# Latent heads of the attention: halves of the output copied by ScalarE and joined by a product with stacked identities

## The chip, the cores and the metric

The kernel runs on one core of a Trainium2 chip. The time is the device time of one execution in microseconds (us), the median of several runs.

## The reference, cut to what matters

One layer of an encoder is computed for two sequences of 512 rows with 1024 columns each: norm and input projection, two groups of attention heads, output projection and residual, then a mixture of 16 experts. Only the attention matters here. It has 16 heads per sequence: 8 grouped-query heads (64 columns, two key/value heads) and 8 latent heads (64 columns plus 32 rotary ones for queries and keys, 64 columns for values, each with keys and values of its own).

```python
def one_block(qblk):
    sc = jnp.einsum('bqkgd,bskd->bkgqs', qblk, k).astype(jnp.float32) * scale
    p = jax.nn.softmax(sc, axis=-1).astype(v.dtype)
    return jnp.einsum('bkgqs,bskd->bqkgd', p, v)
```

## The kernel before

**Stages.** The first stage (project) makes the rows of queries, keys and values of both sequences, the second (attend) does the attention of all 32 heads, g = 0 to 31: the first sequence's 8 grouped and 8 latent heads, then the second's (SETS = 2, HEADS = 16, QH = MH = 8). The third (route) does the output projection, the residual, the norm and the choice of rows for each expert, the fourth the experts.

**Units.** A unit of the attention is one block of 128 queries of one head against its 512 keys, so a head has TS = 4 units and there are NU = 128. Each engine runs through the same counter u, written out by hand, and does for each u one step of several units that are at different ages; semaphores join the engines. For unit u TensorE computes the scores (L1086 and L1087 in grouped heads, three products L1089 to L1091 in latent ones), VectorE takes the negated maximum (L1275), ScalarE the exponential (L1214), TensorE transposes the probabilities (L1100), ScalarE copies them in a rounded format, the high part (L1223), VectorE subtracts it from the transposed probabilities, the low part (L1269). Before a new head, queries and, where it has its own, keys are transposed (L1073) and split in the same way (L1182 to L1188 on ScalarE, L1239 to L1249 on VectorE).

**Values.** Two units at a time, TensorE multiplies values and probabilities (function values, L1118 and L1121). The stationary operand of L1118 has 128 columns, the high part of the values beside their low part. So the bank of PSUM called OT_BANK holds, for one head, 64 rows (0 to 63) from the high part of the values and 64 rows (64 to 127) from the low part, each 512 queries long, and the head's output is the sum of the two, still transposed.

**Joining the halves.** Grouped heads (g % 16 < 8): at u = 4 g + 9 ScalarE copies all 128 rows to the tile ot (L1204) and raises ot_added; at u = 4 g + 10 TensorE multiplies four blocks of it with halves, two 64 x 64 identities one above the other (L463 makes it), which adds the halves and turns them in one (L1133). Latent heads: at u = 4 g + 9 ScalarE copies the lower half to the tile otv (L1206) and raises ot_copied; VectorE adds the upper half from PSUM (L1259, in add_halves, called ahead of the low part of the probabilities, or behind it in the last steps), and raises ot_added; at u = 4 g + 10 TensorE transposes four blocks of 64 rows with an identity (L1135). In both, VectorE then scales the result by the reciprocal of the row sums (L1284, L1287), and SyncE stores groups of heads to HBM.

**Order around it.** On TensorE, in one u: preparations, scores of u, transposes of the probabilities of u - 3, output of a head (u = 4 g + 10), values (u even). Near the end, from u = 125 on, the output projection's first transposes (L1426) and products (L1444) stand in between. The first value product of head g waits until ot_added has counted the g heads before it. Outputs therefore come out some ten steps late: those of heads 6 and 7 (and 22 and 23) while latent heads are scored, those of heads 13 to 15 while grouped heads of the second sequence begin.

Of the kernel before, what the change touches and what calls it, by code (L numbers as in the profile page):

```python
# [16 lines left out]
ALU = mybir.AluOpType  # L17
# [101 lines left out]
def build(nc, a, out):  # L119
# [11 lines left out]
    with ExitStack() as ctx:  # L131
# [107 lines left out]
        att["pthi"] = [Map(shared_at)("probThi0", [P, TS, 2 * P], F32R), bm("probThi1", [P, TS, 2 * P], F32R)]  # L239
        att["v"] = [bm(f"v{i}", [P, TS, 2, VD], F32R) for i in range(2)]  # L240
        att["ot"] = bm("ot", [P, SEQ])
        att["otv"] = bm("otv", [VD, SEQ])
        assert bm.at <= w_in_end, (bm.at, w_in_end)

        om = Map(weights_at)
# [682 lines left out]
def attend(phase, project_signals, a, k, att, wo, ps, banks, o_rows, o_stored, wo_loaded):  # L928
# [23 lines left out]
        due.setdefault(max(0, TS * (g - 1) + (0 if kind == "k" else 2)) if g else -1, []).append((kind, g))  # L952
    PREP, S_BANKS, T_BANKS, OT_BANK, O_BANK = 0, (1, 2, 3), (4, 5), 6, 7
    PAIRS = NU // 2
    pthi, ptlo, ot, otv = (att[n] for n in ("pthi", "ptlo", "ot", "otv"))

    sem = phase.sem
    prep_ready, prep_hi, prep_lo = sem("prep_ready"), sem("prep_hi"), sem("prep_lo")
    score_ready, max_done, exp_done = sem("score_ready"), sem("max_done"), sem("exp_done")
    pt_ready, pthi_done, ptlo_done, pv_done = sem("pt_ready"), sem("pthi_done"), sem("ptlo_done"), sem("pv_done")  # L960
    vhi_done, vlo_done, ot_copied, o_ready, ot_added = sem("vhi_done"), sem("vlo_done"), sem("ot_copied"), sem("o_ready"), sem("ot_added")
    rsum_done, o_done = sem("rsum_done"), sem("o_done")
    wo_hi, wo_scaled, wo_lo = sem("wo_hi"), sem("wo_scaled"), sem("wo_lo")

# [92 lines left out]
    def tensor_program(pe, first_key, finish_tile, o_transposes, product, route_rest):  # L1057
        def prepare(kind, g):
            n = prep_index[kind, g]
            pj, q_rows, kv_rows = rows_of(g)  # L1060
            h = g % HEADS
            if kind == "k":
                wait_for_rows(pe, g)
            if n:
                pe.wait_ge(prep_lo, n)
            for i in range(TS):
                if h < QH:
                    c = h * HD if kind == "q" else C_K + h // GROUP * HD
                    src, dst = pj[:, i, c:c + HD], ps[0:HD, PREP, i * P:(i + 1) * P]
                else:  # L1070
                    src = q_rows[:, i, h - QH, :] if kind == "q" else kv_rows[:, i, h - QH, 0:QK]
                    dst = ps[0:QK, PREP, i * P:(i + 1) * P]
                last = pe.transpose(dst, src, k["ident"][:])  # L1073
            last.then_inc(prep_ready, 1)

        def scores(u):
            g, i = units[u]
            if i == 0:
                pe.wait_ge(prep_lo, prep_index["q", g] + 1)
            if u >= 3:  # L1080
                pe.wait_ge(exp_done, u - 2)
            elif u:
                pe.wait_ge(row_copied, T)
            dst, q, kk, cols = ps[:, S_BANKS[u % 3], :], g % 2, key_of[g] % 2, slice(i * P, (i + 1) * P)
            if g % HEADS < QH:
                pe.matmul(dst, qhi[q][:, cols], khi[kk][:], start=True, stop=False)  # L1086
                last = pe.matmul(dst, qhi[q][:, cols], klo[kk][:], start=False, stop=True)  # L1087
            else:
                pe.matmul(dst, qhi[q][0:QK, cols], khi[kk][0:QK, :], start=True, stop=False)  # L1089
                pe.matmul(dst, qhi[q][0:QK, cols], klo[kk][0:QK, :], start=False, stop=False)  # L1090
                last = pe.matmul(dst, qlo[q][0:QK, cols], khi[kk][0:QK, :], start=False, stop=True)  # L1091
            last.then_inc(score_ready, 1)

        def transpose_probs(u):
            pe.wait_ge(exp_done, u + 1)
            if u >= 2:
                pe.wait_ge(ptlo_done, u - 1)
            for i in range(TS):
                cols = slice(i * P, (i + 1) * P)
                last = pe.transpose(ps[:, T_BANKS[u % 2], cols], att["p"][u % 3][:, cols], k["ident"][:])  # L1100
            last.then_inc(pt_ready, 1)

        def values(m):

            g, qi = units[2 * m]
            pe.wait_ge(ptlo_done, 2 * m + 2)
            if qi == 0:
                pe.wait_ge(vlo_done, key_of[g] + 1)
                if g == 0:
                    pe.wait_ge(kv_done, 3 * T)  # L1110
                if g:
                    pe.wait_ge(ot_added, g)
            v = att["v"][key_of[g] % 2]
            cols = slice(qi * P, (qi + 2) * P)

            for part, i in [("hi", 0)] + [("lo", i) for i in range(TS)] + [("hi", i) for i in range(1, TS)]:
                if part == "hi":
                    last = pe.matmul(ps[:, OT_BANK, cols], v[:, i].rearrange("p a c -> p (a c)"), pthi[m % 2][:, i, :],  # L1118
                                     start=(i == 0), stop=(i == TS - 1))
                else:  # L1120
                    pe.matmul(ps[0:VD, OT_BANK, cols], v[:, i, 0, :], ptlo[m % 2][:, i, :], start=False, stop=False)  # L1121
            last.then_inc(pv_done, 1)

        def transpose_output(g):
            pe.wait_ge(ot_added, g + 1)
            if g:
                pe.wait_ge(o_done, g)
            if g == 0:
                pe.wait_ge(halves_ready, 1)
            for i in range(TS):  # L1130
                dst, cols = ps[:, O_BANK, i * VD:(i + 1) * VD], slice(i * P, (i + 1) * P)
                if g % HEADS < QH:
                    last = pe.matmul(dst, ot[:, cols], k["halves"][:], start=True, stop=True)  # L1133
                else:
                    last = pe.transpose(dst, ot[0:VD, cols], k["ident"][0:VD, 0:VD])  # L1135
            last.then_inc(o_ready, 1)

        first_key()
        prepare("k", 0)
        keys_values = finish_tile(lambda: prepare("q", 0))  # L1140
        for u in range(NU + STEPS):
            if u == 2:
                keys_values(T - 1)
            for kind, g in due.get(u, []):
                prepare(kind, g)
            if u < NU:
                scores(u)
            if 0 <= u - 3 < NU:
                transpose_probs(u - 3)
            if u >= 10 and (u - 10) % TS == 0:  # L1150
                transpose_output((u - 10) // TS)
            if u >= 6 and u % 2 == 0 and (u - 6) // 2 < PAIRS:
                values((u - 6) // 2)
            if u == NU - 3:
                o_transposes(0, 0)
            elif u == NU:
                o_transposes(0, 1)
            elif u == NU + 3:
                product(0, 0)
                product(0, 1)  # L1160
            elif u == NU + 4:
                product(0, 2)
                o_transposes(1, 0)
                product(0, 3)
        route_rest()

    def scalar_program(act, rows, queries, keys_values, o_high, route_rest):
# [27 lines left out]
        for u in range(NU + STEPS):  # L1195
            if u >= 9 and (u - 9) % TS == 0:
                g = (u - 9) // TS
                act.wait_ge(pv_done, TS // 2 * (g + 1))
                if g:
                    act.wait_ge(ot_added, g)  # L1200
                if g % HEADS < QH:
                    if g:
                        act.wait_ge(o_ready, g)
                    act.activation(ot[:], ps[:, OT_BANK, :], ACT.Copy).then_inc(ot_added, 1)  # L1204
                else:
                    act.activation(otv[:], ps[VD:P, OT_BANK, :], ACT.Copy).then_inc(ot_copied, 1)  # L1206
            for kind, g in due.get(u, []):
                prepare(kind, g)
            if 1 <= u <= NU:
# [21 lines left out]
    def vector_program(dve, row_stats, query_stats, key_stats, rb_done, rk_done, o_low, route_rest):  # L1231
# [21 lines left out]
        prepare("k", 0)  # L1253
        prepare("q", 0)
        row_stats(LAST)
        def add_halves(g):
            dve.wait_ge(ot_copied, g // HEADS * MH + g % HEADS - QH + 1)
            dve.wait_ge(o_ready, g)
            dve.tensor_tensor(ot[0:VD, :], ps[0:VD, OT_BANK, :], otv[:], ALU.add).then_inc(ot_added, 1)  # L1259

        for u in range(NU + STEPS):
            halves = (u - 9) // TS if u >= 9 and (u - 9) % TS == 0 and (u - 9) // TS % HEADS >= QH else None
            if halves is not None and u < NU:
                add_halves(halves)
            if 0 <= u - 4 < NU:
                v = u - 4
                dve.wait_ge(pthi_done, v + 1)
                cols = pair_cols(v)
                dve.tensor_tensor(ptlo[v // 2 % 2][:, :, cols], ps[:, T_BANKS[v % 2], :].rearrange("p (a c) -> p a c", a=TS),  # L1269
                                  pthi[v // 2 % 2][:, :, cols].bitcast(F32), ALU.subtract).then_inc(ptlo_done, 1)  # L1270
            if halves is not None and u >= NU:
                add_halves(halves)
            if u < NU:
                dve.wait_ge(score_ready, u + 1)
                dve.tensor_reduce(att["nmax"][:, u:u + 1], ps[:, S_BANKS[u % 3], :], AX.X, ALU.max,  # L1275
# [22 lines left out]
            elif u == NU + 2:  # L1298
                o_low(0, 1)
        route_rest()  # L1300

    attend_signals = {"exp_done": exp_done, "ptlo_done": ptlo_done, "ot_added": ot_added, "o_done": o_done, "score_ready": score_ready,
                      "prep_lo": prep_lo, "pt_ready": pt_ready, "wo_lo": wo_lo, "preps": len(preps)}
    return (sync_program, gpsimd_program, tensor_program, scalar_program, vector_program), attend_signals

# [9 lines left out]
def route(phase, a, x_dram, k, wo, moe, ps, banks, o_rows, out_rows, h2_rows, raw_loaded, o_stored, attend_signals):  # L1315
# [2 lines left out]

    exp_done, ptlo_done, ot_added, o_done, score_ready, prep_lo, pt_ready, wo_lo, preps = (
        attend_signals[n] for n in ("exp_done", "ptlo_done", "ot_added", "o_done", "score_ready", "prep_lo", "pt_ready", "wo_lo", "preps"))
    ORDER = [0, 1, 4, 5, 2, 6, 3, 7]
    PAIRS_DONE = [sum(1 for i in range(TS) if ORDER.index(i) <= j and ORDER.index(TS + i) <= j) for j in range(T)]
    closes = lambda j: PAIRS_DONE[j] > (PAIRS_DONE[j - 1] if j else 0)
# [91 lines left out]
    def tensor_pieces(pe):  # L1417
# [32 lines left out]
        def x_transposes(j, b):  # L1450
            pe.wait_ge(x1_done, 2 * j + b + 1)
            if j:
                pe.wait_ge(x1t_copied, 2 * j - 1 + b)
            else:
                pe.wait_ge(ot_added, ALL)
            for i in range(4):
                c = 4 * b + i
                last = pe.transpose(ps[:, XT[b], i * P:(i + 1) * P], x1[j % 2][:, c * P:(c + 1) * P], k["ident"][:])
# [663 lines left out]
```

## Time and profile before

| | |
|---|---|
| time, median of 3 runs | 1106.7 us (1105.44 to 1107.45) |
| the profiled execution: its own time | 1106.96 us |
| its span | 1105.2 us |
| busy share of the span | TensorE 96%, VectorE 81%, ScalarE 69%, GpSimd 28% |

A matmul instruction is listed on PE and its weight load on PEld; a merged row of the timeline (x4, x8) has the start of the first instruction and the time to the end of the last. Matmuls are pipelined: one starts before the one before it has ended, so the distance between starts is what TensorE needs for it, and the duration is longer.

### The profile page before, as it was taken

How to read it: one execution, taken by the hardware profiler on the slowest of the kernel's cores; microseconds unless marked ns; L12 is line 12 of the kernel's file. 1: busy time of each engine (PE TensorE's matmuls, PEld its weight loads, DVE VectorE, ACT ScalarE, POOL GpSimd, SP SyncE). 2: the span in 40 equal slices, each digit the busy share in tenths (PEclk: the TensorE clock that was granted, in tenths of full speed). 3: DMA queues.
4: the chain of work that ended last, by engine and by line, in shares of the span. 5: the costliest groups of instructions: out<-in, count | busy, mean ns of one | idle time of the engine just before them, and what ended most of it. 6: DMA issues, size and time to landing. Idle time of an engine off the chain costs nothing.

```text
span 1105.2 us, 17052 instructions
## 1 busy us (share of the span) xinstructions
PE 1064.2 (96%) x5795; PEld 908.1 (82%) x5795; DVE 889.9 (81%) x1191; ACT 767.7 (69%) x1033; POOL 309.6 (28%) x338
## 2 busy tenths in 40 slices
PE   8989999999999999999599999999999999999996
PEld 7879978988789888887488888888888888888885
DVE  6777769989998973338898988989889898898982
ACT  8434458888888864443677777777778777787772
POOL 2465557011194712333311101111011110111011
PEclk9999999999999999999799999999999999999998
DMA  8133050010211228551699999999999999999982
GB/s 318 55 119 114 1 204 6 2 39 20 96 40 40 83 70 282 201 203 63 226 419 389 389 388 393 391 415 395 390 390 389 413 395 393 390 390 414 397 303 38
DMA packets 72671, 266.97 MB, mean 242 GB/s; under 512 B 5983, under 2 KB 8122, under 8 KB 72362
## 3 DMA queue, kind: packets, MB, share of 16 engines
q1 hardware_dynamic: 65232, 240.60, 55.7%
q0 software_dynamic: 7328, 25.68, 8.1%
q8 instruction: 30, 0.49, 0.2%
q14 instruction: 23, 0.19, 0.1%
q10 hardware_dynamic: 58, 0.01, 0.0%
HBM read 239.53 MB, written 26.74 MB: 241 GB/s over the span
## 4 chain that ended last, share of the span: by engine, by line
PE 48%; DVE 1%; DMA 1%; issue 0%; ACT 0%; POOLq 0%; POOL 0%; DVEq 0%; ACTq 0%
PE ps L1832 10%; PE ps L1834 10%; PE ps L1833 10%; PE ps L1848 5%; PE ps L1846 5%; PE ps L1847 5%; PE ps L1813 3%; DMA out<-y,give 1%; DMA xe<-h,idxT 0%; DVE idx L1634 0%; DVE affT L1637 0%; DVE gates L1632 0%; ACT hi L1919 0%; DVE lo L1989 0%; POOLq L2069 0%
## 5 line engine op out<-in xcount | busy, mean ns | idle before, releaser
L1989 DVE TENSOR_TENSOR lo<-raw,hi 128x2048 fp32r<-128x2048 f32 x191 | 431.8, 2289 | 56.5 <-ACT hi L1919 47.6
L1919 ACT ACTIVATE hi<-raw 128x2048 fp32r<-128x2048 f32 x192 | 364.5, 1918 | 64.9 <-PE ps L1834 58.9
L1832 PE MATMUL ps<-hi,xehi 128*128 128x512 f32 x480 | 188.1, 392 | 0.2 <-DVE h L2001 0.2
L1834 PE MATMUL ps<-hi,xelo 128*128 128x512 f32 x480 | 186.9, 389 | 0.0
L1833 PE MATMUL ps<-lo,xehi 128*128 128x512 f32 x480 | 186.8, 389 | 0.0
L1768 POOL COPY take<-idxT 128x1 uint32 (+1 forms) x15 | 12.8, 853 | 356.6 <-PE ps L1813 356.6
L1832 PEld LDWEIGHTS ps<-hi,xehi 128*128 128x128 f32 x480 | 90.1, 188 | 18.8 <-issue 0.7
L1834 PEld LDWEIGHTS ps<-hi,xelo 128*128 128x128 f32 x480 | 90.1, 188 | 18.8
L1833 PEld LDWEIGHTS ps<-lo,xehi 128*128 128x128 f32 x480 | 90.2, 188 | 18.2
L1223 ACT ACTIVATE probThi<-ps 128x512 fp32r<-128x512 f32 x128 | 76.2, 595 | 27.9 <-PE ps L1100 27.8
L1846 PE MATMUL ps<-hi,hthi 128*128 128x512 f32 x240 | 94.7, 395 | 0.0
L1269 DVE TENSOR_TENSOR probTlo<-ps,probThi 128x512 fp32r<-128x512 f32 x128 | 87.2, 681 | 8.9 <-ACT probThi L1223 7.6
L1848 PE MATMUL ps<-hi,htlo 128*128 128x512 f32 x240 | 93.5, 390 | 0.0
L1847 PE MATMUL ps<-lo,hthi 128*128 128x512 f32 x240 | 93.4, 389 | 0.0
L1214 ACT ACTIVATE prob<-ps,nmax 128x512 f32<-128x512 f32 x128 | 88.1, 688 | 7.4 <-DVE nmax L1275 6.1
L1275 DVE TENSOR_REDUCE nmax<-ps 128x1 f32<-128x512 f32 x128 | 86.8, 679 | 3.5 <-PE ps L1087 2.1
L1100 PEld LDWEIGHTS ps<-ident,prob 128*128 128x128 f32 x512 | 61.5, 140 | 24.8 <-issue 7.8
L1100 PE MATMUL ps<-ident,prob 128*128 128x128 f32 x512 | 77.2, 273 | 3.1 <-DVE probTlo L1269 2.9
L477 POOL TENSOR_TENSOR small<-small,minus_half 128x1 f32<-128x1 f32 (+4 forms) x40 | 64.9, 1623 | 3.3
L1118 PE MATMUL ps<-probThi,v 128*128 128x256 f32 x256 | 56.9, 304 | 0.0
L1848 PEld LDWEIGHTS ps<-hi,htlo 128*128 128x128 f32 x240 | 45.0, 188 | 9.4
L1847 PEld LDWEIGHTS ps<-lo,hthi 128*128 128x128 f32 x240 | 45.1, 188 | 8.8
(278 smaller groups left out, 2136.3 us busy)
## 6 DMA issues: line engine op xcount, KB each, us to landing
raw<-in_w_gate SPq DMA_DIRECT2D x64, 1024.0 KB, 7.6
raw<-in_w_up SPq DMA_DIRECT2D x64, 1024.0 KB, 7.6
raw<-in_w_down SPq DMA_DIRECT2D x64, 1024.0 KB, 7.5
w_raw<-in_w_in SPq DMA_DIRECT2D x8, 592.0 KB, 8.6
x<-in_x SPq DMA_DIRECT2D x8, 512.0 KB, 4.1
woraw<-in_w_o SPq DMA_DIRECT2D x4, 1024.0 KB, 4.9
o<-attention_out SPq DMA_DIRECT2D x8, 512.0 KB, 4.2
xr<-in_x SPq DMA_DIRECT2D x8, 512.0 KB, 6.3
```

The costliest lines, as they stand in the source:

```text
L1100: last = pe.transpose(ps[:, T_BANKS[u % 2], cols], att["p"][u % 3][:, cols], k["ident"][:])
L1214: act.activation(att["p"][v % 3][:], ps[:, S_BANKS[v % 3], :], ACT.Exp, bias=att["nmax"][:, v:v + 1], accum_out=att["sum"][:, v:v + 1]).th ...
L1269: dve.tensor_tensor(ptlo[v // 2 % 2][:, :, cols], ps[:, T_BANKS[v % 2], :].rearrange("p (a c) -> p a c", a=TS), pthi[v // 2 % 2][:, :, col ...
L1275: dve.tensor_reduce(att["nmax"][:, u:u + 1], ps[:, S_BANKS[u % 3], :], AX.X, ALU.max, negate=True).then_inc(max_done, 1)
L1832: pe.matmul(ps[:, dst[n], :], rowhi[:, c, :], hi[w][:, cols], start=c == 0, stop=False)
L1833: pe.matmul(ps[:, dst[n], :], rowhi[:, c, :], lo[w][:, cols], start=False, stop=False)
L1834: last = pe.matmul(ps[:, dst[n], :], rowlo[:, c, :], hi[w][:, cols], start=False, stop=c == KD - 1)
L1846: pe.matmul(ps[:, Y[n], :], hthi[:, f, :], hi[w][:, cols], start=f == 0, stop=False)
L1847: pe.matmul(ps[:, Y[n], :], hthi[:, f, :], lo[w][:, cols], start=False, stop=False)
L1848: last = pe.matmul(ps[:, Y[n], :], htlo[:, f, :], hi[w][:, cols], start=False, stop=f == KD - 1)
L1919: act.activation(hi[s][:], raw[s][:], ACT.Copy).then_inc(hi_done, 1)
L1989: dve.tensor_tensor(lo[s][:], raw[s][:], hi[s][:].bitcast(F32), ALU.subtract).then_inc(lo_done, 1)
```

## The change

In latent heads ScalarE now does what it does in grouped ones: it copies all 128 rows of the bank to ot, and TensorE multiplies by the stacked identities. The tile otv, the semaphore of the addition and VectorE's addition go; the semaphore ot_added is from here on called ot_copied.

```diff
@@ attend, tensor_program, values
                 if g:
-                    pe.wait_ge(ot_added, g)
+                    pe.wait_ge(ot_copied, g)
@@ transpose_output
-            pe.wait_ge(ot_added, g + 1)
+            pe.wait_ge(ot_copied, g + 1)
...
             for i in range(TS):
                 dst, cols = ps[:, O_BANK, i * VD:(i + 1) * VD], slice(i * P, (i + 1) * P)
-                if g % HEADS < QH:
-                    last = pe.matmul(dst, ot[:, cols], k["halves"][:], start=True, stop=True)
-                else:
-                    last = pe.transpose(dst, ot[0:VD, cols], k["ident"][0:VD, 0:VD])
+                last = pe.matmul(dst, ot[:, cols], k["halves"][:], start=True, stop=True)
@@ scalar_program
                 act.wait_ge(pv_done, TS // 2 * (g + 1))
                 if g:
-                    act.wait_ge(ot_added, g)
-                if g % HEADS < QH:
-                    if g:
-                        act.wait_ge(o_ready, g)
-                    act.activation(ot[:], ps[:, OT_BANK, :], ACT.Copy).then_inc(ot_added, 1)
-                else:
-                    act.activation(otv[:], ps[VD:P, OT_BANK, :], ACT.Copy).then_inc(ot_copied, 1)
+                    act.wait_ge(o_ready, g)
+                act.activation(ot[:], ps[:, OT_BANK, :], ACT.Copy).then_inc(ot_copied, 1)
@@ vector_program
-        def add_halves(g):
-            dve.wait_ge(ot_copied, g // HEADS * MH + g % HEADS - QH + 1)
-            dve.wait_ge(o_ready, g)
-            dve.tensor_tensor(ot[0:VD, :], ps[0:VD, OT_BANK, :], otv[:], ALU.add).then_inc(ot_added, 1)
-
         for u in range(NU + STEPS):
-            halves = (u - 9) // TS if u >= 9 and (u - 9) % TS == 0 and (u - 9) // TS % HEADS >= QH else None
-            if halves is not None and u < NU:
-                add_halves(halves)
...
-            if halves is not None and u >= NU:
-                add_halves(halves)
```

## Rows read from the trace of the kernel before

**Rows 1.** The page: busy time of TensorE, and its granted clock in tenths by slice.

```profile
PE 1064.2 (96%) x5795; PEld 908.1 (82%) x5795; DVE 889.9 (81%) x1191; ACT 767.7 (69%) x1033; POOL 309.6 (28%) x338
...
PEclk9999999999999999999799999999999999999998
```

**Rows 2.** Busy time by stretch: us, PE, PEld, DVE, ACT, POOL (instructions), clock, DMA share, GB/s.

```profile
226.70:267.00 40.30, 40.30 (x290) 35.09 (x288) 36.52 (x66) 33.77 (x76) 5.66 (x10) 1.00 0.11 40
267.00:298.10 31.10, 29.12 (x208) 24.44 (x206) 28.11 (x51) 25.67 (x61) 3.39 (x6) 1.00 0.09 27
...
349.20:389.50 40.30, 40.30 (x290) 35.09 (x288) 36.49 (x65) 33.74 (x76) 29.40 (x22) 1.00 0.21 66
389.50:412.00 22.50, 22.10 (x148) 18.85 (x147) 15.25 (x31) 14.02 (x33) 2.23 (x6) 1.00 0.14 47
412.00:507.00 95.00, 95.00 (x516) 79.47 (x514) 35.66 (x78) 38.73 (x83) 30.84 (x42) 1.00 0.58 206
```

**Rows 3.** Groups by line, 166 to 412 us: busy us, mean ns | idle before, releaser.

```profile
L1133 PE MATMUL ps<-halves,ot 128*128 128x64 f32 x128 | 16.1, 268 | 0.0
...
L1259 DVE TENSOR_TENSOR ot<-ps,otv 64x512 f32<-64x512 f32 x16 | 10.9, 683 | 11.4 <-ACT otv L1206 11.4
L1204 ACT ACTIVATE ot<-ps 128x512 f32<-128x512 f32 x16 | 9.6, 598 | 0.8 <-PE ps L1118 0.8
L1206 ACT ACTIVATE otv<-ps 64x512 f32<-64x512 f32 x16 | 9.5, 596 | 6.6 <-PE ps L1118 6.5
...
L1135 PE MATMUL ps<-ident,ot 64*128 64x64 f32 x64 | 7.3, 235 | 0.0
```

**Rows 4.** Timeline, output groups with products: start us, us, what.

```profile
318.88 1.00 PE L1133 MATMUL ps<-halves,ot 128*128 128x64 f32 x8
...
325.80 1.00 PE L1133 MATMUL ps<-halves,ot 128*128 128x64 f32 x8
...
340.57 0.60 PE L1100 MATMUL ps<-ident,prob 128*128 128x128 f32 x4
341.00 1.00 PE L1133 MATMUL ps<-halves,ot 128*128 128x64 f32 x8
...
349.20 1.00 PE L1133 MATMUL ps<-halves,ot 128*128 128x64 f32 x8
```

**Rows 5.** Timeline, output groups with transposes, second sequence.

```profile
357.51 0.46 PE L1135 MATMUL ps<-ident,ot 64*128 64x64 f32 x4
...
396.61 0.46 PE L1135 MATMUL ps<-ident,ot 64*128 64x64 f32 x4
...
402.56 0.32 PEld L1135 LDWEIGHTS ps<-ident,ot 64*128 64x128 f32 x4 [0.17 <-DVE ot L1259]
...
410.98 0.32 PEld L1135 LDWEIGHTS ps<-ident,ot 64*128 64x128 f32 x4 [0.36 <-issue]
```

**Rows 6.** Timeline, one boundary in a latent head, VectorE and TensorE.

```profile
387.13 0.68 DVE L1259 TENSOR_TENSOR ot<-ps,otv 64x512 f32<-64x512 f32 x1 [0.51 <-ACT otv L1206]
...
387.74 0.67 DVE L1269 TENSOR_TENSOR probTlo<-ps,probThi 128x512 fp32r<-128x512 f32 x1
...
388.33 0.40 PE L1091 MATMUL ps<-khi,qlo 96*128 96x512 f32 x1
...
388.57 0.61 PE L1100 MATMUL ps<-ident,prob 128*128 128x128 f32 x4
...
389.12 0.46 PE L1135 MATMUL ps<-ident,ot 64*128 64x64 f32 x4
```

**Rows 7.** The change of sequences: timeline, and who waited for whom from 267.0 to 298.1.

```profile
266.61 0.46 PE L1135 MATMUL ps<-ident,ot 64*128 64x64 f32 x4
...
297.27 1.00 PE L1133 MATMUL ps<-halves,ot 128*128 128x64 f32 x8
...
ACT prob L1214 <- DVE nmax L1275: 2.2, 6, 0.6
PE ps L1100 <- DVE probTlo L1269: 1.9, 5, 0.5
```

More of the change, by code:

```diff
@@ L241, in build @@
         att["ot"] = bm("ot", [P, SEQ])
-        att["otv"] = bm("otv", [VD, SEQ])
         assert bm.at <= w_in_end, (bm.at, w_in_end)
@@ L954, in attend @@
     PAIRS = NU // 2
-    pthi, ptlo, ot, otv = (att[n] for n in ("pthi", "ptlo", "ot", "otv"))
+    pthi, ptlo, ot = (att[n] for n in ("pthi", "ptlo", "ot"))
     sem = phase.sem
@@ L960, in attend @@
     pt_ready, pthi_done, ptlo_done, pv_done = sem("pt_ready"), sem("pthi_done"), sem("ptlo_done"), sem("pv_done")
-    vhi_done, vlo_done, ot_copied, o_ready, ot_added = sem("vhi_done"), sem("vlo_done"), sem("ot_copied"), sem("o_ready"), sem("ot_added")
+    vhi_done, vlo_done, o_ready, ot_copied = sem("vhi_done"), sem("vlo_done"), sem("o_ready"), sem("ot_copied")
     rsum_done, o_done = sem("rsum_done"), sem("o_done")
@@ L1300, in vector_program @@
         route_rest()
-    attend_signals = {"exp_done": exp_done, "ptlo_done": ptlo_done, "ot_added": ot_added, "o_done": o_done, "score_ready": score_ready,
+    attend_signals = {"exp_done": exp_done, "ptlo_done": ptlo_done, "ot_copied": ot_copied, "o_done": o_done, "score_ready": score_ready,
                       "prep_lo": prep_lo, "pt_ready": pt_ready, "wo_lo": wo_lo, "preps": len(preps)}
@@ L1315, in route @@
 def route(phase, a, x_dram, k, wo, moe, ps, banks, o_rows, out_rows, h2_rows, raw_loaded, o_stored, attend_signals):
-    exp_done, ptlo_done, ot_added, o_done, score_ready, prep_lo, pt_ready, wo_lo, preps = (
-        attend_signals[n] for n in ("exp_done", "ptlo_done", "ot_added", "o_done", "score_ready", "prep_lo", "pt_ready", "wo_lo", "preps"))
+    exp_done, ptlo_done, ot_copied, o_done, score_ready, prep_lo, pt_ready, wo_lo, preps = (
+        attend_signals[n] for n in ("exp_done", "ptlo_done", "ot_copied", "o_done", "score_ready", "prep_lo", "pt_ready", "wo_lo", "preps"))
     ORDER = [0, 1, 4, 5, 2, 6, 3, 7]
@@ L1454, in x_transposes @@
             else:
-                pe.wait_ge(ot_added, ALL)
+                pe.wait_ge(ot_copied, ALL)
             for i in range(4):
```

## The prediction

> **What bounds the kernel now.** I read the page first: TensorE is busy 96% of the span and its clock is granted nearly in full [rows 1], 1.00 in all stretches of rows 2, so the level is 2.4 GHz and the change can't be about the clock. Then busy time by stretch [rows 2]. In the two stretches in which latent heads alone are scored (226.7 to 267.0 and 349.2 to 389.5) TensorE is busy for every one of the 40.3 us, and VectorE for some 36.5. Between them, where the first sequence's last latent outputs meet grouped heads (267.0 to 298.1), TensorE has 2 us of idle time; from 389.5 to 412.0 it has 0.4; from 412.0 to 507.0, the output projection, it is again busy throughout [rows 2]. So a stage of the attention ends when TensorE has issued its work, and what is late at 412 is late at the end: nothing behind it has slack until 507, and the routing that follows waits for the last rows.
>
> Third, the engine detail of one head's boundary [rows 6]. VectorE's addition of the halves starts at 387.13, the low part of the probabilities of that step follows at 387.74 and ends at 388.41, and the transposes of the probabilities that wait for it start at 388.57, right on the heels of the last score product (388.33 plus 0.24): the addition leaves TensorE no idle time to speak of, but it holds these transposes up until the last moment, and the four take 0.55 us to the next group (388.57 to 389.12) instead of the 0.43 of 340.57 to 341.00 [rows 4]. So in an ordinary latent head the addition costs TensorE 0.1 to 0.2 us, though it takes VectorE 0.6.
>
> **The change, part by part.**
>
> Removed: 16 additions of 683 ns on VectorE [rows 3], with the 11.4 us that VectorE idled ahead of them. By themselves worth nothing where VectorE is not last; what TensorE gets back is counted below.
>
> ScalarE: 16 copies of 64x512 (596 ns) become 16 of 128x512 (598 ns) [rows 3]: nothing. The copy now waits for the output's transposes of the head before, which TensorE issued a whole head earlier: nothing. What waits behind the copy on ScalarE, the next exponential, waits no longer than now. The semaphore that lets the next head's value products start comes after the copy and no longer after the addition, some 0.6 us sooner: no loss.
>
> TensorE: 64 transposes with an identity become 64 products with the stacked identities. Each of these is two matmul instructions in the trace (128 for 16 heads, of 268 ns) where a transpose is one (64, of 235 ns) [rows 3]. A group of four lasts 1.00 us instead of 0.46 [rows 4, 6], start to end, so +0.54 us a head before anything is given back. That is the upper bound, 16 x 0.54 = 8.6 us. The lower is what the exchange of 64 instructions of 235 ns for 128 of 268 leaves if all the second ones hide, 64 x 33 ns = 2.1 us, before anything is given back.
>
> The net needs no theory, because two groups of products already stand among latent heads: those of the last two grouped heads come out while latent heads are scored. From 341.00 to 349.20 [rows 4] an interval between output groups holds four latent units, the preparations of a key and a query, and a product group: 8.20 us. That is just what an interval will hold after the change. Today's intervals with transposes, 357.51 to 389.12, are four of 7.90 [rows 5, 6]. So an ordinary latent head gets **0.30 us longer**: 0.54 more work less 0.24 of waiting and of unloaded weights.
>
> Second sequence, by the start of each output group. 349.20 to 357.51 is 8.31 today, since it has the product at its start and the held transposes at its end; it becomes 8.20: -0.11. Then four of +0.30: +1.20, so +1.1 at 389.12. The next three intervals are 7.49, 5.95 and 8.42 [rows 5]; the first has no preparations any more, the second only one unit's scores, the third part of the output projection. In the first TensorE is the bound; in the second the low part of the probabilities is late by way of ScalarE, which follows TensorE and shifts with it, and the wait for the addition (0.17) goes; in the third a wait of 0.36 ahead of the weights hides little. I take +0.30 for each (between 0, were all hidden, and 0.54): +0.90. Last the group at 410.98 itself, +0.45 (0.18 to 0.54, its wait of 0.36 taken off or not). Sum: 1.1 + 0.9 + 0.45 = **+2.45 us**.
>
> First sequence. Up to 266.61 the same as above, +1.1. From 266.61 to 297.27 [rows 7] three heads' outputs come out while grouped heads begin: 30.66 us for four intervals. Here TensorE does wait: five times for the low part of the probabilities, 1.9 us in all by the profile, in a stretch with fewer score products and VectorE with the addition on top. With the addition gone VectorE has the work of a grouped head, for which the interval is 6.92 (318.88 to 325.80) [rows 4], and TensorE is then the bound. The four become 8.20, then 6.92 with one unit's third score product (0.23 to 0.24, the distance from 388.33 to 388.57 [rows 6]) = 7.15, then 6.92 twice: 29.19, so -1.47. Sum: 1.1 - 1.47 = **-0.4 us**. Bounds: -1.47 if they are fully paid back, or +1.5 (three more groups at 0.5, nothing given back) if these waits are not the addition's.
>
> Sum -0.4 + 2.45 = **+2.1 us**. The profiled execution took 1106.96 us (span 1105.2 and 1.8 around it) and would take 1109.1; it lies 0.3 above the median of 1106.7, for which I say 1108.8.
>
> The Trainium skill ("Perfetto Trace Analysis", section Optimizing Tensor Performance) says that a logical transpose should be done as a transpose and not as a standard matmul; its rule speaks against this change, and by it alone the sum would be the 8.6 us above; the 8.20 against 7.90 of the rows makes it a little over half of that in the ordinary heads.
>
> The same page (section Optimizing Scalar/DVE Operations) says that work can be moved from VectorE if VectorE is saturated. By it the 16 additions would be worth up to 9.6 us (0.6 each); the stretches of rows 2 with TensorE busy throughout say otherwise, and the rival below prices it.
>
> **Rivals.**
>
> *The waits at the change of sequences stay (slower).* The five waits of 267 to 298 are put down to the low part of the probabilities, which itself waits for ScalarE's high part. If it is ScalarE's order (copy of the output, then exponential, then high part) that makes it late, taking away the addition gives nothing and those four intervals cost 1.5 more instead of 1.47 less: +2.1 + 3.0 = +5.1, or about +3.6 if half stays: 1110.3 to 1111.8. For: the exponentials too wait there for VectorE's maximum, six times [rows 7], so both engines are in the ring. Against: VectorE idles ahead of nearly every addition until ScalarE's copy is done (11.4 us for 16 of them [rows 3]), so the addition brings a wait of its own into the ring besides its 0.6 us, and grouped heads with the same ScalarE copy and no addition run at 6.92. It decides from about +0.3 us over my sum, since that already is over 0.2%.
>
> *VectorE paces the latent heads (faster).* If the addition held back the whole ring and the second matmul instructions hid, the 13 ordinary intervals would fall by the 0.24 that the addition holds TensorE up, -3.1, and the change of sequences by the whole 1.9 of its waits: -5, 1101.7. It is the case of the skill's rule on VectorE. Point of decision: a product group costing TensorE less than 0.24 more. Against: TensorE has no idle time in those stretches, and 8.20 against 7.90 is measured with everything else alike.
>
> *Hidden at the end.* The last groups stand beside the output projection, where the rows of another tile are still loading. If all of the last +1.35 is hidden: +0.75, 1107.4. Against: busy throughout from 412 on.
>
> That the product costs otherwise than in grouped heads is hardly possible: shapes and operands are those of the 64 there.
>
> **How the numbers follow.** About 0.2% (2.2 us) is what a measurement of this kernel can tell from no change, and +2.1 lies just inside it. Chances: my sum, between +1.2 and +3, 0.68; waits stay 0.17; hidden at the end 0.10; VectorE 0.05. Of the first case half falls below +2.2, given that the three runs shown spread over 2 us; the second is slower, the third the same. So faster 0.05, same 0.46, slower 0.49. The likeliest is 1108.8. The range goes from +0.75 with some spread of the runs, 1107.0, to the half-kept waits with the same, 1111.2. The likeliest case alone reaches from 1107.9 to 1109.9.
>
> **What would show it.** Right: 256 matmul instructions of products with the stacked identities and no transposes of the output; intervals in latent heads of 8.20; from the last of them in the first sequence to the first grouped one about 29.2 us over four intervals; no wait of TensorE for the low part of the probabilities in 267 to 298; VectorE's busy time down by 11 us, TensorE's up by 5 or more; the start of the routing's last stretch about 2 us later, and the experts' stretch as long as now. Wrong: intervals in latent heads under 7.9 (VectorE paced them), or waits of 0.3 and more still there in the change of sequences, or a projection stretch that takes up the shift.

## The result, and the profile after

The changed kernel took 1108.61 us (median of 14 runs, 1107.36 to 1111.3) against 1106.79 us of the kernel before (14 runs, 1105.15 to 1108.25): ratio 1.0018, 95% interval 1.0011 to 1.0025. It is slower by 1.8 us, clear of zero, and by just under the 0.2% that I had set as the line. The forecast was 1108.8.

The two profiled executions lie only 0.3 us apart in span (1105.5 after, 1105.2 before). That is chance and can be taken out. The output group of a head is the run of four products or transposes that turns its output. The group of head 7, the last grouped head, starts at 225.13 in the profile after and at 226.73 in the one before, and up to there both run the same instructions. (Other edits of the kernel after start it at 224.86, 226.71 and 229.15.) From there on intervals are compared.

Busy time by stretch of the kernel after, columns as in [rows 2]:

```profile
226.70:267.00 40.30, 40.30 (x297) 36.74 (x295) 34.28 (x59) 31.58 (x75) 5.65 (x10) 1.00 0.11 40
267.00:298.10 31.10, 31.10 (x235) 28.29 (x234) 27.75 (x50) 24.95 (x62) 3.39 (x6) 1.00 0.16 55
...
349.20:389.50 40.30, 40.30 (x297) 36.77 (x296) 34.13 (x59) 32.06 (x74) 27.37 (x21) 1.00 0.21 66
389.50:412.00 22.50, 22.09 (x155) 19.84 (x153) 11.85 (x23) 12.45 (x30) 2.22 (x6) 1.00 0.14 48
412.00:507.00 95.00, 95.00 (x517) 79.69 (x515) 35.82 (x78) 38.72 (x83) 30.60 (x42) 1.00 0.59 206
```

TensorE now is busy for all 31.1 us of the change of sequences, where it had 2 us of idle time [rows 2]. In the two stretches of 40.3 us and from 412 on it was busy throughout before and is so now, and from 389.5 to 412.0 it has 0.4 us of idle time as before; there what came in could only lengthen something.

Two signs of the forecast did not come. On the page TensorE's busy time is up by 2.9 us (1064.2 to 1067.1) and not by 5 or more, and VectorE's is down by 6.6 (889.9 to 883.3) and not by 11. Busy time is merged, so where TensorE was busy throughout it can only grow with the span. From head 7's group to the product behind head 31's it grows by 3.9 (182.0 to 185.9): the 1.9 by which this stretch is longer and the 2 us of idle time that are filled; ahead of head 7 the chance of the start takes 1.9 off again. VectorE's busy time in the same stretch falls by 6.4 (162.5 to 156.1) and not by the additions' 10.9, since the records of its instructions overlap where they are close (387.13 plus 0.68, the next from 387.74 [rows 6]) and with more room overlap less.

Groups by line from 166 to 412 us, columns as in [rows 3]:

```profile
L1131 PE MATMUL ps<-halves,ot 128*128 128x64 f32 x256 | 32.1, 268 | 0.0
...
L1197 ACT ACTIVATE ot<-ps 128x512 f32<-128x512 f32 x32 | 19.1, 598 | 8.0 <-PE ps L1117 8.0
```

All 32 heads go the same way: 256 matmuls of 268 ns, 32 copies of 598 ns. Output groups of the timeline, in the second sequence and around the change of sequences:

```profile
347.10 1.00 PE L1131 MATMUL ps<-halves,ot 128*128 128x64 f32 x8
...
355.30 1.00 PE L1131 MATMUL ps<-halves,ot 128*128 128x64 f32 x8
...
388.10 1.00 PE L1131 MATMUL ps<-halves,ot 128*128 128x64 f32 x8
...
395.88 1.00 PE L1131 MATMUL ps<-halves,ot 128*128 128x64 f32 x8
...
402.13 1.00 PE L1131 MATMUL ps<-halves,ot 128*128 128x64 f32 x8
...
410.85 1.00 PE L1131 MATMUL ps<-halves,ot 128*128 128x64 f32 x8
411.66 0.48 PE L1425 MATMUL ps<-wohi,othi 128*128 128x512 f32 x1
...
266.13 1.00 PE L1131 MATMUL ps<-halves,ot 128*128 128x64 f32 x8
...
295.15 1.00 PE L1131 MATMUL ps<-halves,ot 128*128 128x64 f32 x8
```

347.10 to 388.10 is five intervals of 8.20. They were 39.92 together [rows 4 to 6]. 266.13 to 295.15 is 29.02, where it was 30.66 [rows 7]. The last three intervals are 7.78, 6.25 and 8.72, each 0.29 to 0.30 more than in [rows 5, 6]. The product of the output projection behind the last group (L1425, before L1444) starts 0.81 after it, where it started 0.39 after it:

```profile
411.37 0.73 PE L1444 MATMUL ps<-wohi,othi 128*128 128x512 f32 x2
```

(This row is of the kernel before; the group ahead of it is the last of [rows 5].)

And the waits from 267.0 to 298.1 (engine line, what it waited for: us in total, times, longest), all those with VectorE in them:

```profile
DVE probTlo L1252 <- ACT probThi L1214: 1.8, 5, 0.5
...
ACT prob L1205 <- DVE nmax L1256: 0.4, 2, 0.2
DVE nmax L1256 <- PE ps L1090: 0.3, 1, 0.3
```

The wait of TensorE for the low part, five times before [rows 7], is gone, and it is now VectorE that waits for ScalarE.

The account from head 7's group to the last: +1.12 (39.88 to 41.00, heads 7 to 12), -1.64 (heads 12 to 16), +0.02 (16 to 23, grouped), +1.08 (23 to 28), +0.89 (28 to 31), and +0.42 for the last group: **+1.89 us**, against +1.82 in the medians. It arrives whole at the experts: their first products on the new activations start 319.77 us after head 7's group (544.90), where it was 317.78 (544.51), +1.99.

```profile
544.90 0.47 PE L1813 MATMUL ps<-hi,hthi 128*128 128x512 f32 x1 [1.02 <-issue]
```

```profile
544.51 0.47 PE L1832 MATMUL ps<-hi,hthi 128*128 128x512 f32 x1 [1.02 <-issue]
```

### The profile page after: what moved, and what is told of

It reads as the page before. It is cut to its first block, busy times and chain, and to the rows that moved or that the text cites. A ratio compares the mean times of both kernels' runs of the same rounds, so it can differ in the third digit from the quotient of the medians.

```text
span 1105.5 us, 17148 instructions
## 1 busy us (share of the span) xinstructions
PE 1067.1 (97%) x5859; PEld 917.0 (83%) x5859; DVE 883.3 (80%) x1175; ACT 763.6 (69%) x1033; POOL 311.5 (28%) x338
## 4 chain that ended last, share of the span: by engine, by line
PE 48%; DVE 1%; DMA 1%; issue 1%; ACT 0%; POOLq 0%; POOL 0%; DVEq 0%; ACTq 0%
PE ps L1813 10%; PE ps L1815 10%; PE ps L1814 10%; PE ps L1829 5%; PE ps L1827 5%; PE ps L1828 5%; PE ps L1794 3%; DMA out<-y,give 1%; DMA xe<-h,idxT 0%; DVE idx L1615 0%; DVE affT L1618 0%; DVE gates L1613 0%; ACT hi L1900 0%; DVE lo L1970 0%; POOLq L2050 0%
```

## The experiments

All of them are edits of the kernel before or after; each was timed in five rounds beside the kernel before. The table has the ratio to the kernel before, the median, and four numbers of one profile each: an ordinary latent interval (first / second sequence where they differ), the four intervals from head 12 to head 16 (the change of sequences), the time from head 7's group to head 31's, and the span less the start of head 7's group, which leaves out what varies ahead of the change. The kernel before, timed anew each time, had medians of 1106.79 to 1107.03.

```
                       ratio (95%)             median   ordinary  12 to 16  7 to 31  span less 7
before                                                  7.90      30.66     184.25   878.5
after                  1.0018 (1.0011-1.0025)  1108.61  8.20      29.02     185.72   880.4
first sequence only    0.9988 (0.9979-0.9997)  1105.90  8.20/7.90 29.03     183.72   877.9
second sequence only   1.0019 (1.0010-1.0028)  1109.07  7.90/8.20 30.66     186.28   880.3
no addition            0.9973 (0.9960-0.9986)  1103.91  7.88      28.30     181.70   875.5
addition and product   1.0071 (1.0057-1.0085)  1115.43  8.55      31.63     192.37   887.0
heads 13 to 15 only    0.9980 (0.9971-0.9988)  1104.21  7.90      28.67     182.26   876.2
wide transposes        0.9987 (0.9978-0.9996)  1105.06  7.76      30.59     182.69   876.6
turn, then add         0.9977 (0.9967-0.9987)  1104.26  7.73/7.80 30.64     182.53   876.1
the same, all heads    1.0053 (1.0040-1.0066)  1111.76  7.73/7.80 30.64     186.84   881.8
addition later         0.9987 (0.9978-0.9996)  1105.15  7.88      29.29     182.67   876.7
load alone             1.0024 (1.0013-1.0034)  1109.36  8.20      29.52     186.22   881.5
wait alone             1.0010 (1.0001-1.0020)  1108.57  8.20      29.10     185.75   880.4
both findings          0.9960 (0.9946-0.9973)  1101.78  7.76      28.68     180.77   874.6
```

**Where it comes from: one sequence at a time.** A list in the kernel says which heads take the new way; the others keep copy, addition and transposes.

```diff
+    JOINED = [g for g in range(ALL) if g % HEADS < QH or QH <= g < HEADS]
...
-                if g % HEADS < QH:
+                if g in JOINED:
                     last = pe.matmul(dst, ot[:, cols], k["halves"][:], start=True, stop=True)
```

> The change in the first sequence's eight latent heads (8 to 15) alone. Theory (ordinary latent head 0.3 us longer, change of sequences 1.6 us shorter): intervals between output groups of 8.20 from head 8 on, the four intervals from head 12 to head 16 29.0 us instead of 30.66, the second sequence as before (7.90), time about -0.5 us against before. Rival (each of the 16 heads costs the same 0.11 us): +0.9 us. Rival (the first sequence's waits are ScalarE's, and the gain seen was chance): +1 us or more.

Measured: ratio 0.9988, intervals 8.20 in the first sequence and 7.90 in the second, 29.03 at the change of sequences: 0.5 us less from head 7 to head 31. The other half has `g >= HEADS + QH` in the list.

> The change in the second sequence's eight latent heads (24 to 31) alone. Theory: the first sequence as before with 30.66 us from head 12 to head 16, then 8.20 instead of 7.90, 0.3 more in each of the last three intervals and 0.4 for the last group: +2.4 us. Rival (each head costs the same): +0.9 us. Rival (hidden behind the output projection's loads at the end): +1.1 us.

Measured: ratio 1.0019; 30.66 at the change of sequences, 8.20 in the second sequence, and 2.03 us more from head 7 to head 31 with 0.4 for the last group behind it. The same edit makes one sequence faster and the other slower. "Every head costs the same" fell, and so did "hidden at the end".

**What the addition costs.** The addition is taken out, and ScalarE copies the upper half alone, so the low part of the values is left out of the latent heads' result; the transposes stay.

```diff
-                    act.activation(otv[:], ps[VD:P, OT_BANK, :], ACT.Copy).then_inc(ot_copied, 1)
+                    act.wait_ge(o_ready, g)
+                    act.activation(ot[0:VD, :], ps[0:VD, OT_BANK, :], ACT.Copy).then_inc(ot_added, 1)
...
-            dve.tensor_tensor(ot[0:VD, :], ps[0:VD, OT_BANK, :], otv[:], ALU.add).then_inc(ot_added, 1)
```

> The addition is left out and the transposes are kept: ScalarE copies the upper half alone to the tile that is transposed, so the low part of the values is left out of the latent heads' result. It tells what VectorE's addition by itself costs the path. Theory: the addition costs TensorE 0.1 to 0.15 us in an ordinary head and most of 3.3 us at the change of sequences (27.3 us instead of 30.66 from head 12 to head 16), intervals of 7.77 instead of 7.90: about -5 us. Rival (VectorE paces the latent heads): up to -9.6 us, intervals of 7.3. Rival (the waits at the change of sequences are ScalarE's): about -2 us, with waits for the low part of the probabilities still there.

Measured: ratio 0.9973, 2.55 us less from head 7 to head 31: of these 2.36 at the change of sequences (30.66 to 28.30) and 0.02 in each ordinary head (7.90 to 7.88). I had expected 7.77. In an ordinary head, then, the addition costs next to nothing, and the transposes of the probabilities (L1100) are slow without it too. Timeline of this kernel at an ordinary boundary, TensorE and its weight loads:

```profile
386.07 0.59 PEld L1100 LDWEIGHTS ps<-ident,prob 128*128 128x128 f32 x4
386.30 0.60 PE L1100 MATMUL ps<-ident,prob 128*128 128x128 f32 x4
...
386.83 0.32 PEld L1135 LDWEIGHTS ps<-ident,ot 64*128 64x128 f32 x4 [0.16 <-issue]
386.83 0.46 PE L1135 MATMUL ps<-ident,ot 64*128 64x64 f32 x4
```

The weights of the probabilities are loaded 0.23 ahead (386.07 for 386.30), nothing holds them up, and still the output group starts 0.53 behind them, with 0.16 of idle time ahead of its own weights. It is the output group that comes late, not the group ahead of it.

**The price of the product alone.** The addition stays and the 64 rows are multiplied by the identity instead of transposed.

```diff
-                    last = pe.transpose(dst, ot[0:VD, cols], k["ident"][0:VD, 0:VD])
+                    last = pe.matmul(dst, ot[0:VD, cols], k["ident"][0:VD, 0:VD], start=True, stop=True)
```

> The addition is kept, and the transpose of the 64 rows becomes a product with the same 64x64 identity: TensorE's price alone, with nothing given back. Theory: 0.43 us a head in the ordinary heads (8.33 instead of 7.90, the transposes of the probabilities ahead of it still held up), partly absorbed in the waits at the change of sequences: +5 to +7 us. Rival (the 0.24 us that the changed heads get back comes of the product's own weight loads and not of the addition): intervals of 8.20, and +3 us or less.

Measured: ratio 1.0071, intervals of 8.55 where I had expected 8.33, 8.12 us more from head 7 to head 31: more than either expectation. At the change of sequences it is 0.97 more (30.66 to 31.63), less than four such heads cost elsewhere, since part of it falls into the waits. Timeline of this kernel at one group:

```profile
395.50 0.61 PE L1100 MATMUL ps<-ident,prob 128*128 128x128 f32 x4
...
396.04 0.96 PEld L1135 LDWEIGHTS ps<-ident,ot 64*128 64x128 f32 x8 [0.17 <-issue]
...
396.04 1.10 PE L1135 MATMUL ps<-ident,ot 64*128 64x64 f32 x8
...
397.08 0.39 PE L1118 MATMUL ps<-probThi,v 128*128 128x256 f32 x1
```

A product with 64 rows takes 1.04 us from its start to the next group, one with all 128 rows 0.81 or 0.82 (341.00 in [rows 4] to 341.82). The group is also reached late: 0.54 from the start of the transposes ahead of it (395.50 for 396.04), where it is 0.43 in [rows 4]. Half as many rows are dearer. So the change gained something that has nothing to do with VectorE: it uses all 128 rows.

**Where the addition is felt: heads 13 to 15.** The list of the first experiment, with `13 <= g <= 15`.

> The change in heads 13, 14 and 15 alone, whose outputs come out at the change of sequences; the other 13 latent heads keep addition and transposes. Theory (the addition costs TensorE nothing where four latent units are scored, and over 2 us at the change of sequences): intervals of 7.90 everywhere else, 28.5 to 28.7 us from head 12 to head 16 instead of 30.66, so -2 us against before, faster than both kernels. Rival (the waits there go only if VectorE is relieved from head 8 on): 30 us or more for these four intervals and no gain.

Measured: ratio 0.9980, 28.67 us for the four intervals, 1.99 less from head 7 to head 31, the rest as before. The relief is needed only there, and in the other 13 heads the change has a price and no return.

**64 rows against 128.** The addition stays; all 128 rows of ot are transposed in latent heads.

```diff
-                    last = pe.transpose(dst, ot[0:VD, cols], k["ident"][0:VD, 0:VD])
+                    last = pe.transpose(ps[:, O_BANK, cols], ot[:, cols], k["ident"][:])
```

> Addition kept; in latent heads all 128 rows of the tile are transposed with the 128x128 identity instead of 64 rows with the 64x64 one (the lower 64 rows hold an old head's and are not read). It asks why the product, with 0.44 us more on TensorE by starts, lengthened an ordinary head by only 0.30 to 0.32. Theory (weights of 64 rows are not loaded ahead of the instruction before them, which costs 0.1 us on entering and leaving the group): intervals of 7.78 instead of 7.88 to 7.90, the idle time of 0.17 ahead of the group's weights gone, about -1.5 us in all. Rival (it is transposes against products, not the row count): 7.90 to 7.95 and the 0.17 still there, 0 to +0.8 us.

Measured: ratio 0.9987, intervals of 7.76, 1.56 us less. Timeline at a boundary of this kernel:

```profile
240.63 0.42 PEld L1100 LDWEIGHTS ps<-ident,prob 128*128 128x128 f32 x4 [0.23 <-issue]
240.67 0.62 PE L1100 MATMUL ps<-ident,prob 128*128 128x128 f32 x4
241.02 0.47 PEld L1135 LDWEIGHTS ps<-ident,ot 128*128 128x128 f32 x4
241.12 0.60 PE L1135 MATMUL ps<-ident,ot 128*128 128x128 f32 x4
```

Here the addition is back and the weights of L1100 are late again (0.23 idle), but the output group follows after 0.45 and its weights are loaded 0.1 ahead. In the kernel without the addition it is the other way round, and yet the interval is the shorter one here. Twice the data transposed, 0.14 us less a head.

**Load, place or wait at the change of sequences.** ScalarE copies all rows, TensorE transposes them, and VectorE adds the halves of the turned output behind them:

```diff
+                    turned = ps[:, O_BANK, :].rearrange("p (i a c) -> p i c a", i=TS, a=2)
+                    dve.tensor_reduce(out, turned, AX.X, ALU.add).then_inc(o_added, 1)
...
+                    dve.tensor_tensor(out, out, scale, ALU.mult).then_inc(o_done, 1)
```

> ScalarE copies all 128 rows as in the changed kernel, TensorE transposes all 128 rows instead of multiplying, and VectorE adds the two halves of the turned output from PSUM behind it (a reduction over pairs, 128x256 out of 128x512) ahead of the scaling; latent heads only. It tells whether what hurts at the change of sequences is VectorE's load or that the addition stands ahead of the low part of the probabilities, where ScalarE's copy holds it up. Theory (its place and its wait for the copy): ordinary intervals 7.78, and 28 to 29 us from head 12 to head 16, about -3.5 us against before. Rival (VectorE's load alone): ordinary 7.78, but 30 us or more there, -1.5 us or less.

Measured: ratio 0.9977 and 7.73 to 7.80 in ordinary heads, but 30.64 at the change of sequences. My theory of 28 to 29 there fell, and the rival (the load) had the number. VectorE's work is much the same, 0.69 us for 0.68, its place another, and it hurts as much there as with the addition and transposes of all rows (30.59):

```profile
281.45 0.69 DVE L1278 TENSOR_REDUCE pjB<-ps 128x256 f32<-128x512 f32 x1
282.17 0.42 DVE L1280 TENSOR_TENSOR pjB<-pjB,rsum 128x256 f32<-128x256 f32 x1
282.51 0.68 DVE L1257 TENSOR_TENSOR probTlo<-ps,probThi 128x512 fp32r<-128x512 f32 x1
```

It stands right ahead of a low part again, and TensorE waits for low parts three times in this stretch, 2.8 us in all:

```profile
PE ps L1101 <- DVE probTlo L1257: 2.8, 3, 1.1
```

> The same as the run before, in grouped heads too, where it replaces 64 more products. Theory (TensorE is the bound in grouped heads, by little): 0.2 to 0.38 us less in each of 16 grouped intervals (6.55 to 6.7 instead of 6.92), -3 to -6 us against the run before, -6 to -9 against the kernel before. Rival (VectorE becomes the bound in grouped heads, with 0.68 us more each): 6.9 or more, no gain over the run before, or a loss.

Measured: ratio 1.0053; grouped intervals of 7.65 and more instead of 6.92, as the rival said and not my theory. The 0.73 more is about what was added to VectorE, 0.69. Groups by line of this kernel, 180 to 214 us, show who waits: TensorE for the low part, ScalarE for the maximum, both VectorE's.

```profile
L1210 ACT ACTIVATE prob<-ps,nmax 128x512 f32<-128x512 f32 x18 | 12.5, 694 | 5.4 <-DVE nmax L1261 5.4
...
L1101 PE MATMUL ps<-ident,prob 128*128 128x128 f32 x68 | 10.3, 273 | 4.2 <-DVE probTlo L1257 4.2
```

So in grouped heads VectorE has no 0.7 us to spare, and TensorE's product is the right way there.

**The order alone.** The kernel before, with the addition behind the low part of its step in all heads, where it already stood in the last steps:

```diff
-            if halves is not None and u < NU:
+            if halves is not None and u < 0:
...
-            if halves is not None and u >= NU:
+            if halves is not None and u >= 0:
```

> The kernel before, with VectorE's addition moved behind the low part of the probabilities of its step. It takes away the order (the low part no longer stands behind the addition and behind the wait for ScalarE's copy) and leaves the load. Theory now (VectorE's load at the change of sequences, nothing in ordinary heads): intervals of 7.90, 30.4 to 30.7 us from head 12 to head 16, the time within 0.5 us of before. Rival (the order): 7.78 in ordinary heads and 29.5 us or less there, -2 us or more.

Measured: ratio 0.9987, 7.88 in ordinary heads, 29.29 at the change of sequences. Neither side's number: nothing in ordinary heads, as said, but 1.37 of the 2.36 us that the addition costs at the change of sequences go with its place. What is left, 1.0, is the load together with its wait for ScalarE's copy, which now stands ahead of the maximum.

**The load alone and the wait alone**, in the changed kernel, heads 13 to 15:

```diff
+            if u in (4 * 13 + 9, 4 * 14 + 9, 4 * 15 + 9):
+                some = k["tab"][:].rearrange("p t c -> p (t c)")[0:VD, 0:SEQ]
+                dve.tensor_tensor(att["otv"][:], some, some, ALU.add)
```

> The changed kernel, with one VectorE addition of 64x512 that nobody waits for and that waits for nobody (a table added to itself) at the place of the old addition in heads 13, 14 and 15. Theory (the load): 30.0 to 30.7 us from head 12 to head 16 instead of 29.02, so +1.0 to +1.6 us against the changed kernel, 1109.6 to 1110.3. Rival (the wait for ScalarE's copy or the order of semaphores): 29.0 to 29.2 and no difference from the changed kernel, 1108.6.

Measured: 29.52 instead of 29.02, less than my theory's 30.0, and all of it in one interval (8.67 instead of 8.18), the one in which this instruction took 1.05 us instead of 0.67:

```profile
274.12 1.05 DVE L1251 TENSOR_TENSOR otv<-tab 64x512 f32<-64x512 f32 x1
```

The other two took 0.67 and the intervals stayed as they were. This stand-in is not quite the old addition. It reads a table and nothing from PSUM, and in all three places it met an instruction of GpSimd, one of the two being longer than otherwise. GpSimd's L1051 ran from 273.90 to 274.63 beside the one of 1.05. Its L1049 took 0.83 and 0.87 beside the other two, where it takes 0.40 in the kernel before:

```profile
273.90 0.73 POOL L1051 TENSOR_TENSOR v<-kv_rowsB,v 128x256 fp32r<-128x256 f32 x1
...
281.40 0.67 DVE L1251 TENSOR_TENSOR otv<-tab 64x512 f32<-64x512 f32 x1
...
281.50 0.83 POOL L1049 CAST v<-pj 128x256 fp32r<-128x256 f32 x1 [6.87 <-PE ps L1118]
```

The old addition, which reads one input from PSUM, took 0.68 beside the same L1051 (272.39 and 273.00 in the kernel before). So the 0.5 us look like the price of this meeting and not of 0.68 us of load; no run without GpSimd's instruction shows it.

```diff
+            if u in (4 * 13 + 9, 4 * 14 + 9, 4 * 15 + 9):
+                dve.wait_ge(ot_copied, (u - 9) // TS + 1)
```

> The changed kernel, in which VectorE in heads 13, 14 and 15 waits for ScalarE's copy of the output ahead of the low part of the probabilities, as it had to for the addition, and does nothing else for it. Theory (most of what the addition cost at the change of sequences is this wait in front of the low part): 29.5 to 30.2 us from head 12 to head 16 instead of 29.02, with waits of TensorE for the low part back, +0.5 to +1.2 us against the changed kernel. Rival (wait and work cost only together): 29.0 to 29.2 and no difference.

Measured: 29.10, 0.08 more, and no difference in the time from the changed kernel (1108.57). VectorE does wait there, and nobody notices:

```profile
DVE probTlo L1254 <- ACT ot L1197: 1.5, 3, 0.6
```

So my expectation fell: the wait by itself is hidden, the work by itself nearly so. The likeliest reading is that both together, the addition behind its wait and ahead of the low part, use up the slack that VectorE has there; the changed kernel with both was not run. In these two kernels the output group is a product and keeps TensorE 0.4 us longer, so VectorE also has that much more time. That may be why what was left in the run before costs 1.0 and the load here at most 0.5; it was argued and not tested.

**Both findings together.** Product in heads 13 to 15, and elsewhere the addition with transposes of all rows.

> Both findings together: the product in heads 13 to 15, where VectorE is the bound, and in the other 13 latent heads the addition with transposes of all 128 rows. Theory: 7.76 in ordinary heads and 28.4 to 28.6 us from head 12 to head 16, about -3.5 us against before, 1103.4, faster than both kernels. Rival (the gains overlap): no better than either alone, -2 us.

Measured: ratio 0.9960 (0.9946 to 0.9973), 1101.78 us: faster than both kernels, 3.48 us less from head 7 to head 31, the sum of the two (1.99 and 1.56). The median says 5.1 us; the span less head 7's start says 3.9.

## Why the prediction was right, and where a step of it was not

**The ordinary heads.** +0.30 a head from the interval 341.00 to 349.20 [rows 4]: measured 8.20 in every one of them. It worked because the profile already held an interval with all that the change would put into it.

**Its explanation failed.** The sum had "0.54 more work less 0.24 of waiting and of unloaded weights", and put that on the addition holding up the transposes of the probabilities. Without the addition the interval is 7.88, so the addition's share is 0.02. The late group was the output's own, and it is late with 64 rows: with 128 rows transposed it is 7.76 with the addition still there. Between starts, the product takes 0.43 more than the transposes (0.82 against 0.39), and 0.12 comes back with the rows. The same holds of the interval 349.20 to 357.51 and of the last ones. The 8.31 that the forecast put down to held-up transposes is still 8.29 to 8.30 without the addition, and the 5.95 and 8.42 are unchanged, so the 0.17 read as a wait for VectorE [rows 5] was the late weight load, and the 0.36 no wait for it either. The number was right since the precedent has 128 rows as well; had I priced the product with 64 rows from the same precedent I would have been 0.35 us a head short, as the run with 8.55 shows.

**The change of sequences.** Forecast 29.19, measured 29.02, of which 28.30 is what is left with neither addition nor product. That the addition holds TensorE up there, and that taking it away more than pays for the products, was right; the intervals of grouped heads came within 0.1 us (7.06, 6.87 and 6.91 for 7.15, 6.92 and 6.92). The rival that those waits are ScalarE's fell with the five waits gone and with the run without the addition. Its bound of +1.5 was rough too: it counts three groups where four (heads 12 to 15) lie in these intervals.

**The end.** +0.30 each for the last three intervals, measured +0.29, +0.30 and +0.30; +0.45 for the last group, measured +0.42. Nothing was hidden there: "hidden at the end" fell. The sum, +2.1, against +1.9 in the profile and +1.8 in the medians: the largest piece of the difference is the change of sequences, 0.17 better than forecast. Two sums beside it don't quite come out: half of 0.68 with the other cases gives 0.44 for the same and 0.51 for slower, not 0.46 and 0.49, and +3 on 1106.7 is 1109.7 and not 1109.9.

**"VectorE paces the latent heads"** fell in all runs: with VectorE relieved of 11 us in the kernel without addition, 2.55 us are gained, 2.36 of them in four intervals. The busy share would not have told where: VectorE was busy for 91% of the stretches in which an ordinary head gains 0.02, and for 90% of the change of sequences [rows 2]. The Trainium skill ("Perfetto Trace Analysis", section Optimizing Scalar/DVE Operations) advises moving work to another engine when VectorE is saturated. Here that paid in 3 of 16 heads, those where TensorE waited for VectorE. What the same page of the Trainium skill says on transposes (section Optimizing Tensor Performance) agrees with the trace in direction: the transposes of 128 rows take 0.36 from their start to the next group (241.12 to 241.48), the product 0.82.

## What to carry to other kernels

When a change is made in all places alike, ask where its gain is and where its price: here the gain lay in 3 heads of 16 and the price in all of them, and the part of the edit that pays (heads 13 to 15) makes the kernel 2 us faster by its profile (2.7 by the medians) where the whole makes it 1.8 slower. Look in the profile for an interval that already holds what the change will bring; it gives the net without a theory, though it doesn't tell why. And where an instruction with 64 rows stands between others with 128 on TensorE, time it with 128 before taking the smaller one to be cheaper.

## What the runs showed of the hardware that I had not expected

Output groups with 64 rows have their weights loaded late: 0.16 to 0.17 us of idle time ahead of the load in each one (0.36 in the last one), none where the shape is 128 rows. It is not every row count under 128: the score products with 96 rows have their weights loaded ahead (388.11 for 388.33 in the kernel before).

```profile
388.11 0.19 PEld L1091 LDWEIGHTS ps<-khi,qlo 96*128 96x128 f32 x1
```

What about 64 rows does it was not tried. Four transposes of 128 rows shorten the interval to 7.76, four of 64 rows leave it at 7.88 to 7.90, and four products of 64 rows take 1.04 us where those of 128 rows take 0.82.

The runs of one kernel spread over 1.4 to 4.9 us, and in the profiles much of this lies ahead of the attention's latent heads: head 7's group started at 224.9 to 229.2 us in fourteen profiles whose code is the same up to there or differs little. Measured from that group on, profiles agree with the account of their intervals to 0.7 us, and for edits of 1 or 2 us that was of more use than the time of a single run.
